# One waiting rule for a prefetched slab, and a weight split moved up on VectorE, in a two-block transformer kernel on one core

## The chip, the cores and the metric

The kernel runs on one core of a Trainium2 chip. The core has five engines with a queue of instructions each: TensorE (PE in the profile, with its weight loads as PEld), VectorE (DVE), ScalarE (ACT), GpSimd (POOL) and SyncE (SP), which in this kernel only issues DMAs. The engines meet through semaphores. The metric is the device time of one execution in microseconds, lower is better. Differences are judged against the kernel before, run on the same chip.

## The reference

Two transformer blocks in float32 over 256 tokens of width 1024. Cut to what matters here:

```python
# block 1
xn = rmsnorm(x, norm1_w)
gq, gk, gv, ggate, gr, mq, mk, mv = split(xn @ w_in)
o_gla  = rmsnorm(gla_chunked(gq, gk, gv, log_a), gla_out_norm_w) * silu(ggate)   # 4 heads
o_moba = moba_attention(rope(rmsnorm(mq)), rope(rmsnorm(mk)), mv)                # 8 heads, causal
x = x + (concat(o_gla, o_moba) * mix_scale) @ w_out
x = x + peer_ffn(rmsnorm(x, norm2_w), ...)        # 128 x 128 experts, top 16 of 8 heads
# block 2, for l in (0, 1): all of its scales and shifts come from
mod = silu(c) @ ada_w[l] + ada_b[l]               # 1024 x 6144 for each l
x = layer_norm(ALPHA * x + g1 * mixer(modulate(x, sh1, sc1)))
x = layer_norm(ALPHA * x + g2 * mlp(modulate(x, sh2, sc2)))
```

The product `silu(c) @ ada_w` depends on nothing that block 1 computes. The kernel computes pieces of it, called ada rows below, between the steps of block 1.

## The kernel before, in words

**Weights.** Every weight matrix comes in tiles of 128x1024 floats (512 KB). SP loads tile n into one of four places of `raw`, once tile n-4 has been split (`load`, L369). ACT rounds each half tile (128x512) to `w_hi` (`hi`, run under L1114), DVE computes the rest `w_lo = raw - w_hi` (`lo`, L1613), and TensorE multiplies three products of hi and lo parts (L497, L498). `w_hi` and `w_lo` hold four halves. DVE signals each finished half on `lo_done`.

**The ada rows.** One ada row (512 outputs) needs four slabs of `ada_w` of 128x1024 floats, slabs 4k to 4k+3 for row k. They lie in a ring of `ADA_RING = 4` places in `route`. `ada(k, ...)` (L574) makes eight products of 512 columns, two for each slab; before the first product of a slab TensorE waits for that slab's DMA (`ada_full`), and after it `ada_started` is counted up by one; after the eighth product of the row, `ada_row_full` is counted up by one. So `ada_started >= m` says that the first product of slab m-1 is done, and `ada_row_full >= k+1` that row k is done. `load_ada(n)` (L381 to L388) on SP waits until the slab's place is free and issues its DMA:

```python
if n % ADA_BATCH == ADA_BATCH - 1:
    sp.wait_ge(s["ada_row_full"], n // ADA_BATCH)       # fourth slab of a row: the row before is done
else:
    sp.wait_ge(s["ada_started"], n + 2 - ADA_RING)      # slab n-3 has begun, so slab n-4 is done
```

Rows 0 to 5 (slabs 0 to 23) run in block 1. SP's queue is strictly in order and mixes slabs with weight tiles: slabs 4 to 7 stand between the second and the third tile of `gg`, slabs 8 to 11 between the second and the third tile of `mv`, slabs 12 to 15 between the second and the third tile of `w_out`, slabs 16 to 23 ahead of the last four tiles of `w_out`.

**Order on TensorE, stage by stage.** ... ada row 0, `mk` projection, state updates (L670), rope rotations (L676), **ada row 1**, `gg` projection, gated linear attention output (`go`, L691 and L698), **ada row 2**, `mv` projection, then the softmax attention over four units of two heads (u = 0 to 3). For a unit, `moba_scores` (L735, L738), `moba_transposes` (L748) and `moba_values` (L764, L767). Between these stand **ada row 3** in two halves, the products `gbc` (L776) for the norm of the linear attention, and **rows 4 and 5** in halves. `ada_columns` (L567) and the `w_out` projection follow.

**Order on DVE in that last stage.** `moba_shifted(u)` (L1768 to L1775) scales and masks the scores and takes the maximum; ACT then does the exponentials; `moba_scaled(u)` (L1781, L1785) divides by the sum and releases the transposes of unit u on TensorE. L1807 multiplies the linear attention by `gbc` and frees the four PSUM banks of `gbc` (two of which the transposes of unit 0 take, the other two the scores of unit 2); L1814 applies the gate. `mixed_low` (L1792) and `moba_mixed` (L1798) prepare the input of `w_out`. The program is written out by hand; there is no scheduler.

Of the kernel before, what the change touches and what calls it, by code (L numbers as in the profile page):

```python
# [38 lines left out]
ADA_RING = 4  # L39
ADA_BATCH = 4  # L40
# [13 lines left out]
def columns(*sized):  # L54

    at, where = 0, {}
    for name, n in sized:
        where[name] = (at, n)
        at += n
    return where, at  # L60
# [14 lines left out]
TILE, NTILE = columns(("gq", 2), ("gk", 2), ("gr", 1), ("gv", 4), ("mq", 4), ("mk", 4), ("gg", 4), ("mv", 4),  # L75
                      ("w_out", KC), ("wq", 16), ("u", P), ("v", P),
                      ("aq", 4), ("ak", 4), ("bq", 4), ("bk", 1), ("av", 4), ("bv", 1), ("w_out2", KC),
                      ("mlp0", 64), ("conv_u", 16), ("conv_gate", 8), ("conv_out", KC), ("mlp1", 64))
# [46 lines left out]
def build(nc, ins, out):  # L125
    with ExitStack() as ctx:
# [26 lines left out]
        s = {name: ctx.enter_context(nc.semaphore(name)) for name in SEMS}  # L153
        raw_full = [ctx.enter_context(nc.semaphore(f"raw_full{i}")) for i in range(RAW)]
        ada_full = [ctx.enter_context(nc.semaphore(f"ada_full{i}")) for i in range(ADA_RING)]
# [4 lines left out]
        def V(name, i=0):  # L160
            return vec[:, VEC[name][0] + i:VEC[name][0] + i + 1]
# [27 lines left out]
        def C1(name):  # L189
            return con1[:, CON1[name][0]:CON1[name][0] + CON1[name][1]]  # L190
# [83 lines left out]
        ada_w = route[:, 0:ADA_RING * D]  # L274
# [3 lines left out]
        ada_slots = [ada_w[:, k * D:(k + 1) * D] for k in range(ADA_RING)]  # L278
# [11 lines left out]
        def use(name, k=0):  # L290
            n = USE[name][0] + k
            return n % NBANK, n // NBANK

        def B(name, k=0):
            return bank[use(name, k)[0]]

        def wait_full(eng, name, k=0, more=0):
            b, n = use(name, k)
            eng.wait_ge(bank_full[b], more + (n + 1))

        def wait_freed(eng, name, k=0, more=0):

            b, n = use(name, k)
            eng.wait_ge(bank_free[b], more + (n + 1))
# [23 lines left out]
        def free(name, k=0):  # L328
            return bank_free[use(name, k)[0]]

        def unit(n, half):

            a = (2 * n + half) % UNITS * HALF
            return slice(a, a + HALF)
# [10 lines left out]
        def ada_slot(n):  # L345

            r = n if n < ADA_1 * ADA_BATCH else n - ADA_GATES * ADA_BATCH
            return r % ADA_RING, r // ADA_RING
# [20 lines left out]
        def _(sp):  # L369
# [8 lines left out]
                for q in range(q0, TILE[name][1] if q1 is None else q1):  # L378
                    load(name, q, src[first + q])

            def load_ada(n, slot_free=False):  # L381
                if n >= ADA_RING and not slot_free:
                    if n % ADA_BATCH == ADA_BATCH - 1:
                        sp.wait_ge(s["ada_row_full"], n // ADA_BATCH)
                    else:
                        sp.wait_ge(s["ada_started"], n + 2 - ADA_RING)
                slot = ada_slot(n)[0]
                sp.dma_start(ada_slots[slot], ins["ada_w"][n]).then_inc(ada_full[slot], 16)  # L388

            def looped(name, src):  # L390
                with sp.Fori(0, TILE[name][1] // ROUND) as i:
# [7 lines left out]
            for name in ("gq", "gk", "gr", "gv", "mq", "mk"):  # L399
                straight(name, ins["w_in"], at)  # L400
                at += TILE[name][1]
                if name == "gv":
                    for n in range(ADA_RING):
                        load_ada(n)
            for n, name in enumerate(("gg", "mv")):
                straight(name, ins["w_in"], at, q1=2)
                for m in range(ADA_RING):
                    load_ada((n + 1) * ADA_RING + m)
                straight(name, ins["w_in"], at, q0=2)
                at += TILE[name][1]  # L410
            straight("w_out", ins["w_out"], q1=2)
            for n in range(3 * ADA_RING, 4 * ADA_RING):
                load_ada(n)
# [1178 lines left out]
        def _(dve):  # L1592
# [3 lines left out]
            def step(ins):  # L1596
                steps[0] += 1
                ins.then_inc(s["dve_step"], 1)
# [5 lines left out]
            def then_wait(ins):  # L1604
                step(ins)
                settle()

            def lo(n, i=0):

                for half in range(2):  # L1610
                    dve.wait_ge(s["hi_done"], i * (2 * ROUND) + (2 * n + half + 1))
                    a = n % RAW * D + half * HALF
                    v.tensor_tensor(w_lo[:, unit(n, half)], raw[:, a:a + HALF], w_hi[:, unit(n, half)].bitcast(F32),  # L1613
                                    ALU.subtract).then_inc(s["lo_done"], 1)
# [147 lines left out]
            def moba_shifted(u):  # L1762

                c = (u % 2) * 16
                for m in range(2):
                    a = (u % 2) * 6 * P + m * 3 * P
                    wait_full(dve, f"mp{u}", m)
                    v.scalar_tensor_tensor(sm1[:, a:a + 3 * P], B(f"mp{u}", m)[:, 0:3 * P], HD ** -0.5, C1("causal"),  # L1768
                                           ALU.mult, ALU.add).then_inc(free(f"mp{u}", m), 1)
                for m in range(2):  # L1770
                    wait_freed(dve, f"mp{u}", m)
                both = sm1[:, (u % 2) * 6 * P:(u % 2 + 1) * 6 * P].rearrange("p (m c) -> p m c", m=2)
                step(v.tensor_reduce(smx[:, c:c + 2], both[:, :, 0:P], AX, ALU.max))
                then_wait(v.tensor_reduce(smx[:, c + 2:c + 4], both[:, :, P:3 * P], AX, ALU.max))
                v.tensor_scalar(smx[:, c + 4:c + 8], smx[:, c:c + 4], -1.0, None, ALU.mult).then_inc(s["sm1_max"], 1)  # L1775

            def moba_scaled(u):

                c = (u % 2) * 16
                dve.wait_ge(s["sm1_exp"], u + 1)  # L1780
                then_wait(v.reciprocal(smx[:, c + 12:c + 16], smx[:, c + 8:c + 12]))  # L1781
                both = sm1[:, (u % 2) * 6 * P:(u % 2 + 1) * 6 * P].rearrange("p (m c) -> p m c", m=2)
                for n, part in enumerate((both[:, :, 0:P], both[:, :, P:3 * P])):
                    w = part.shape[2]
                    last = v.tensor_tensor(part, part, smx[:, c + 12 + 2 * n:c + 14 + 2 * n].unsqueeze(2).to_broadcast([P, 2, w]), ALU.mult)  # L1785
                last.then_inc(s["sm1_p"], 1)
# [12 lines left out]
                    .then_inc(s["chunk_t"], 1)  # L1799

            moba_shifted(0)
            moba_shifted(1)
            moba_scaled(0)
            for hd in range(GLA_H):
                a = slice((hd % 2) * 512 + (hd // 2) * T, (hd % 2) * 512 + (hd // 2) * T + T)
                wait_full(dve, "gbc", hd)
                v.tensor_tensor(mixed[:, hd * T:(hd + 1) * T], o_gla[:, a], B("gbc", hd)[:, 0:T], ALU.mult)\  # L1807
                    .then_inc(free("gbc", hd), 1)
            for hd in range(GLA_H):
                a = slice(hd * T, (hd + 1) * T)  # L1810
                if hd % 2 == 0:
                    wait_freed(dve, "gg", hd // 2)
                wait_freed(dve, "gbc", hd)
                v.scalar_tensor_tensor(mixed[:, a], mixed[:, a], V("mix", hd), gg[:, a], ALU.mult, ALU.mult).then_inc(s["chunk_t"], 1)  # L1814
            moba_shifted(2)
            moba_scaled(1)
            lo(TILE["w_out"][0] + 1)
            for c in range(4):
                mixed_low(c)
            moba_shifted(3)  # L1820
# [648 lines left out]
```

## Time and profile before

| | us |
|---|---|
| median of 3 executions | 1798.35 |
| lowest, highest | 1795.98, 1800.77 |
| the profiled execution: its time | 1800.77 |
| the profiled execution: span from first to last instruction | 1799.0 |

| engine | busy us | share | instructions |
|---|---|---|---|
| PE | 1704.0 | 95% | 11514 |
| DVE | 1215.2 | 68% | 2417 |
| ACT | 951.3 | 53% | 1830 |
| POOL | 77.2 | 4% | 74 |

The span is the time between the first and the last instruction of the profiled execution; about 1.8 us of its own time lie outside it. Busy shares are means over the whole span, with very different stages under them, so a local change is read in its own stage: here the stretch from 60 to 160 us. The granted clock of TensorE is 0.984 of full over the span.

### The profile page before, as it was taken

To read this page: it belongs to the slowest core of one execution; us is meant where nothing else is said; L and a number is where in the kernel's file an instruction comes from. 1 tells how busy PE (TensorE), PEld (TensorE's weight loads), DVE (VectorE), ACT (ScalarE), POOL (GpSimd) and SP (SyncE) were. 2 spreads that over 40 slices of the span, in tenths; PEclk is the share of its full clock that TensorE was granted. 3 is DMA by queue.
4 is the path that set the end of the run, shared out by engine and by line. 5 is a ranking of instruction groups with operands and counts; after the bars stand their busy time and mean duration, and the time that the engine had idled before them with its cause. 6 is when DMAs were issued, how large, how long until landed. Compare 5 with 4: busy or idle time off the path is not lost.

```text
span 1799.0 us, 33460 instructions
## 1 busy us (share of the span) xinstructions
PE 1704.0 (95%) x11514; PEld 1511.0 (84%) x11514; DVE 1215.2 (68%) x2417; ACT 951.3 (53%) x1830; POOL 77.2 (4%) x74
## 2 busy tenths in 40 slices
PE   7999999999999888999999999988999999889997
PEld 6767999999999755688888888867899979889996
DVE  5556568878854599866666676467676666767666
ACT  5445454554554588555555564346554445445443
POOL 0000000000000166200000000000000000000000
PEclk9989999999999899999999999999999999999999
DMA  6654445555555587565665654400365554445553
GB/s 235 213 206 166 146 151 181 175 186 175 176 185 180 194 291 281 190 195 191 203 208 191 193 192 138 163 24 14 118 187 186 187 208 150 149 137 188 187 188 101
DMA packets 86934, 316.35 MB, mean 176 GB/s; under 512 B 9664, under 2 KB 9808, under 8 KB 86352
## 3 DMA queue, kind: packets, MB, share of 16 engines
q1 hardware_dynamic: 85248, 309.30, 52.6%
q10 hardware_dynamic: 1328, 4.01, 0.6%
q0 software_dynamic: 288, 2.10, 0.3%
q8 instruction: 45, 0.74, 0.2%
q14 instruction: 25, 0.20, 0.0%
HBM read 314.32 MB, written 1.05 MB: 175 GB/s over the span
## 4 chain that ended last, share of the span: by engine, by line
PE 88%; DVE 6%; issue 2%; ACT 2%; DMA 1%; ACTq 0%; POOLq 0%; DVEq 0%; SPq 0%
PE bank L497 31%; PE acc L497 21%; PE bank L498 15%; PE acc L498 10%; PE bank L855 4%; PE acc L574 2%; PE bank L595 1%; ACT arena L1114 1%; DVE w_lo L1613 1%; DVE small L2110 1%; ACT w_hi L1114 1%; PE bank L814 0%; ACT L1114 0%; DVE arena L2131 0%; PE acc L980 0%
## 5 line engine op out<-in xcount | busy, mean ns | idle before, releaser
L1613 DVE TENSOR_TENSOR w_lo<-raw,w_hi 128x512 fp32r<-128x512 f32 x982 | 652.4, 689 | 421.6 <-ACT w_hi L1114 419.8
L1114 ACT ACTIVATE w_hi<-raw 128x512 fp32r<-128x512 f32 x982 | 592.5, 627 | 389.8 <-PE acc L497 239.1
L497 PE MATMUL bank<-x_hi,w_hi 128*128 128x256 f32 x2224 | 636.2, 286 | 23.2 <-DVE w_lo L1613 16.2
L497 PE MATMUL bank<-x_lo,w_hi 128*128 128x256 f32 x2224 | 632.3, 284 | 0.0
L498 PE MATMUL bank<-x_hi,w_lo 128*128 128x256 f32 x2224 | 632.1, 284 | 0.0
L497 PEld LDWEIGHTS bank<-x_hi,w_hi 128*128 128x128 f32 x2224 | 429.1, 193 | 30.7 <-issue 16.1
L497 PEld LDWEIGHTS bank<-x_lo,w_hi 128*128 128x128 f32 x2224 | 429.4, 193 | 0.8 <-issue 0.2
L498 PEld LDWEIGHTS bank<-x_hi,w_lo 128*128 128x128 f32 x2224 | 429.2, 193 | 0.0
L1114 ACT ACTIVATE arena<-bank 128x256 f32<-128x256 f32 (+4 forms) x172 | 89.6, 527 | 293.2 <-PE bank L498 291.6
L497 PE MATMUL acc<-w_hi,x_hi 128*128 128x512 f32 x560 | 219.3, 392 | 3.9 <-DVE w_lo L1613 2.5
L497 PE MATMUL acc<-w_lo,x_hi 128*128 128x512 f32 x560 | 218.4, 390 | 0.0
L498 PE MATMUL acc<-w_hi,x_lo 128*128 128x512 f32 x560 | 218.2, 390 | 0.0
L497 PEld LDWEIGHTS acc<-w_hi,x_hi 128*128 128x128 f32 x560 | 105.3, 188 | 30.5 <-issue 5.0
L498 PEld LDWEIGHTS acc<-w_hi,x_lo 128*128 128x128 f32 x560 | 105.3, 188 | 21.9
L497 PEld LDWEIGHTS acc<-w_lo,x_hi 128*128 128x128 f32 x560 | 105.3, 188 | 21.2
L855 PEld LDWEIGHTS bank<-route 128*128 128x128 f32 x512 | 62.8, 196 | 50.3 <-issue 50.2
L1574 POOL TENSOR_TENSOR route<-route,small 128x512 f32<-128x512 f32 x64 | 71.8, 1123 | 661.9 <-DVE route L1956 661.9
L497 PE MATMUL acc<-w_hi,tail_r 128*128 128x512 f32 x256 | 99.9, 390 | 0.0
L497 PE MATMUL acc<-w_lo,tail_r 128*128 128x512 f32 x256 | 99.9, 390 | 0.0
L498 PE MATMUL acc<-w_hi,tail_r 128*128 128x512 f32 x256 | 99.7, 389 | 0.0
L855 PE MATMUL bank<-route 128*128 128x128 f32 x512 | 71.7, 290 | 19.0 <-issue 17.5
L1956 DVE TENSOR_TENSOR route<-con,small 128x512 f32<-128x512 f32 x83 | 79.1, 971 | 0.0
(257 smaller groups left out, 1554.9 us busy)
## 6 DMA issues: line engine op xcount, KB each, us to landing
raw<-in_peer_u SPq DMA_DIRECT2D x128, 512.0 KB, 3.5
raw<-in_peer_v SPq DMA_DIRECT2D x128, 512.0 KB, 3.6
raw<-in_mlp_w SPq DMA_DIRECT2D x128, 512.0 KB, 3.5
ada_x<-in_ada_w SPq DMA_DIRECT2D x64, 512.0 KB, 4.1
route<-in_ada_w SPq DMA_DIRECT2D x32, 512.0 KB, 5.5
raw<-in_w_in SPq DMA_DIRECT2D x25, 512.0 KB, 4.5
raw<-in_conv_w_in SPq DMA_DIRECT2D x24, 512.0 KB, 4.1
raw<-in_attn_w_in SPq DMA_DIRECT2D x18, 512.0 KB, 3.4
```

Source lines behind the costliest of these rows:

```text
L497: return (mm(dst, a[0], b[0], start=start, stop=False, **kw), mm(dst, a[0], b[1], start=False, stop=False, **kw), mm(dst, a[1], b[0], star ...
L498: mm(dst, a[1], b[0], start=False, stop=stop, **kw))
L574: return mm(row[g:g + ADA_COLS, :], sc[:, a:a + ADA_COLS], w, start=start, stop=False, skip_group_check=True)
L595: last = mm(ps[:, 0:T], C("mean_d"), src[:, c, :], start=(c == 0), stop=(c == KC - 1))
L855: last = mm(ps[:, t * P:(t + 1) * P], jone[:, b:b + P], ione[:, a:a + P], start=True, stop=True)
L1114: return nc.scalar.activation(dst, src, f, **kw)
L1574: nc.gpsimd.tensor_tensor(e, e, gT[:, bass.ds(i * 32 + 4 * g, 4)].unsqueeze(2).to_broadcast([P, 4, P]), ALU.mult).then_inc(s["gated_i"], 1)
L1613: v.tensor_tensor(w_lo[:, unit(n, half)], raw[:, a:a + HALF], w_hi[:, unit(n, half)].bitcast(F32), ALU.subtract).then_inc(s["lo_done"], 1)
L1956: return v.tensor_tensor(dst.rearrange("p (t k) -> p t k", t=4), C("iota").unsqueeze(1).to_broadcast(shape), index[:, bass.ds(token, 4)].u ...
L2110: step(v.tensor_reduce(smx[:, c + m:c + m + 1], B(f"sc{n}_{m}")[:, :], AX, ALU.max))
```

## The change

Two edits. First, `load_ada` waits by one rule for every slab: `ada_started >= n-2`. (Its new argument `i` is never given and adds zero.) Second, on DVE the split of the second `w_out` tile moves from behind `moba_scaled(1)` to behind `moba_shifted(0)`, and `moba_scaled(0)` moves behind the four multiplications by `gbc`.

```diff
-            def load_ada(n, slot_free=False):
+            def load_ada(n, i=0, slot_free=False):
                 if n >= ADA_RING and not slot_free:
-                    if n % ADA_BATCH == ADA_BATCH - 1:
-                        sp.wait_ge(s["ada_row_full"], n // ADA_BATCH)
-                    else:
-                        sp.wait_ge(s["ada_started"], n + 2 - ADA_RING)
+
+                    sp.wait_ge(s["ada_started"], i * ADA_RING + (n + 2 - ADA_RING))
                 slot = ada_slot(n)[0]
-                sp.dma_start(ada_slots[slot], ins["ada_w"][n]).then_inc(ada_full[slot], 16)
+                sp.dma_start(ada_slots[slot], ins["ada_w"][i * ADA_RING + n]).then_inc(ada_full[slot], 16)
...
             moba_shifted(0)
+            lo(TILE["w_out"][0] + 1)
             moba_shifted(1)
-            moba_scaled(0)
             for hd in range(GLA_H):
...
+            moba_scaled(0)
             for hd in range(GLA_H):
...
             moba_shifted(2)
             moba_scaled(1)
-            lo(TILE["w_out"][0] + 1)
             for c in range(4):
                 mixed_low(c)
```

SP's queue around the slabs of rows 1 to 5, with what each DMA waits for; first before, then after. `route<-in_ada_w` is a slab, `raw<-in_w_in` and `raw<-in_w_out` are weight tiles.

```order
L375 DMA raw<-in_w_in 128x1024 [waits lo_done] x10
L388 DMA route<-in_ada_w 128x1024 [waits ada_started] x3
L388 DMA route<-in_ada_w 128x1024 [waits ada_row_full]
L375 DMA raw<-in_w_in 128x1024 [waits lo_done] x4
L388 DMA route<-in_ada_w 128x1024 [waits ada_started] x3
L388 DMA route<-in_ada_w 128x1024 [waits ada_row_full]
L375 DMA raw<-in_w_in 128x1024 [waits lo_done] x2
L375 DMA raw<-in_w_out 128x1024 [waits lo_done] x2
```

```order
L375 DMA raw<-in_w_in 128x1024 [waits lo_done] x10
L386 DMA route<-in_ada_w 128x1024 [waits ada_started] x4
L375 DMA raw<-in_w_in 128x1024 [waits lo_done] x4
L386 DMA route<-in_ada_w 128x1024 [waits ada_started] x4
L375 DMA raw<-in_w_in 128x1024 [waits lo_done] x2
L375 DMA raw<-in_w_out 128x1024 [waits lo_done] x2
```

No DMA changes its place; the fourth slab of each row waits for another semaphore. The order on TensorE is the same before and after.

VectorE in the attention stage, from `moba_shifted(0)` on; first before, then after (line numbers are lower by two). The TENSOR_TENSOR into `w_lo` is the weight split, the row with `arena,bank 128x256 x4` the multiplications by `gbc`.

```order
L1775 TENSOR_SCALAR small<-small 128x4
L1768 SCALAR_TENSOR_TENSOR arena<-bank,arena 128x384 x2
L1773 TENSOR_REDUCE small<-arena 128x2
L1774 TENSOR_REDUCE small<-arena 128x2
L1775 TENSOR_SCALAR small<-small 128x4
L1781 RECIPROCAL small<-small 128x4
L1785 TENSOR_TENSOR arena<-arena,small 128x2x128
L1785 TENSOR_TENSOR arena<-arena,small 128x2x256
L1807 TENSOR_TENSOR arena<-arena,bank 128x256 x4
L1814 SCALAR_TENSOR_TENSOR arena<-arena,vec 128x256 x4
```

```order
L1773 TENSOR_SCALAR small<-small 128x4
L1611 TENSOR_TENSOR w_lo<-raw,w_hi 128x512 x2
L1766 SCALAR_TENSOR_TENSOR arena<-bank,arena 128x384 x2
L1771 TENSOR_REDUCE small<-arena 128x2
L1772 TENSOR_REDUCE small<-arena 128x2
L1773 TENSOR_SCALAR small<-small 128x4
L1805 TENSOR_TENSOR arena<-arena,bank 128x256 x4
L1779 RECIPROCAL small<-small 128x4
L1783 TENSOR_TENSOR arena<-arena,small 128x2x128
L1783 TENSOR_TENSOR arena<-arena,small 128x2x256
L1813 SCALAR_TENSOR_TENSOR arena<-arena,vec 128x256 x4
```

Two splits and four multiplications now stand ahead of the scaling that releases the first transposes. No instruction is added or removed.

## Rows read from the trace of the kernel before

**Rows 1.** The page: engines of the chain that ended last.
```profile
PE 88%; DVE 6%; issue 2%; ACT 2%; DMA 1%; ACTq 0%; POOLq 0%; DVEq 0%; SPq 0%
```

**Rows 2.** Timeline of PE, the ada rows (start us, us, instruction, count).
```profile
84.21 1.92 PE L574 MATMUL acc<-route,small 128*32 128x512 f32 x16
...
107.04 3.64 PE L574 MATMUL acc<-route,small 128*32 128x512 f32 x16
...
127.41 1.07 PE L574 MATMUL acc<-route,small 128*32 128x512 f32 x8
...
129.27 1.06 PE L574 MATMUL acc<-route,small 128*32 128x512 f32 x8
130.26 1.27 PE L776 MATMUL bank<-arena,norm_rows 32*128 32x256 f32 x8
133.72 0.85 PE L748 MATMUL bank<-con,arena 128*128 128x128 f32 x6 [2.19 <-DVE arena L1807]
...
136.37 1.07 PE L574 MATMUL acc<-route,small 128*32 128x512 f32 x8
```

**Rows 3.** Timeline of SP's queue, 60 to 165 us.
```profile
69.81 2.03 SPq L388 DMA_DIRECT2D route<-in_ada_w  x4
72.30 15.89 SPq L375 DMA_DIRECT2D raw<-in_w_in  x4
88.24 1.94 SPq L388 DMA_DIRECT2D route<-in_ada_w  x4
```

**Rows 4.** Timeline of SP's queue, a narrow window: slab 20 alone.
```profile
137.51 0.33 SPq L388 DMA_DIRECT2D route<-in_ada_w  x1
```

**Rows 5.** DMA issues: 137.4 to 142.2 us, and all 32 slabs (L388).
```profile
route<-in_ada_w SPq DMA_DIRECT2D x1, 512.0 KB, 3.4
...
DMA to landing us min/median/max: 3.4/5.5/11.0
```

**Rows 6.** Timeline of ACT: the rounding of the third `gg` and `mv` tiles.
```profile
87.97 0.63 ACT L1114 ACTIVATE w_hi<-raw 128x512 fp32r<-128x512 f32 x1
...
113.89 1.17 ACT L1114 ACTIVATE w_hi<-raw 128x512 fp32r<-128x512 f32 x2
```

**Rows 7.** Timeline of DVE in the attention stage.
```profile
129.76 1.01 DVE L1768 SCALAR_TENSOR_TENSOR arena<-bank,arena 128x384 f32<-128x384 f32 x2
...
132.01 0.17 DVE L1781 RECIPROCAL small<-small 128x4 f32<-128x4 f32 x1
...
133.16 1.41 DVE L1807 TENSOR_TENSOR arena<-arena,bank 128x256 f32<-128x256 f32 x4
134.48 1.67 DVE L1814 SCALAR_TENSOR_TENSOR arena<-arena,vec 128x256 f32<-128x256 f32 x4
136.07 1.02 DVE L1768 SCALAR_TENSOR_TENSOR arena<-bank,arena 128x384 f32<-128x384 f32 x2
...
139.46 1.29 DVE L1613 TENSOR_TENSOR w_lo<-raw,w_hi 128x512 fp32r<-128x512 f32 x2
```

**Rows 8.** The chain that ended last, in order of time.
```profile
143.19 5.58 DMA route<-in_ada_w
148.81 1.05 PE acc L574 x4
```

**Rows 9.** Stretches: us, busy time of PE, PEld, DVE, ACT, POOL, clock, DMA.
```profile
101.50:110.60 9.10, 9.10 (x36) 4.94 (x34) 0.00 (x0) 0.00 (x0) 0.00 (x0) 0.50 0.00 0
...
41.60:50.00 8.40, 5.78 (x25) 4.43 (x24) 4.26 (x7) 6.31 (x15) 0.00 (x0) 1.00 0.77 267
...
612.80:616.10 3.30, 0.03 (x1) 0.03 (x1) 1.18 (x4) 1.92 (x3) 0.00 (x0) 1.00 0.83 278
616.10:627.20 11.10, 9.61 (x37) 4.97 (x38) 8.89 (x15) 8.12 (x23) 7.00 (x6) 0.54 0.56 202
...
181.10:183.60 2.50, 0.02 (x1) 0.00 (x0) 2.38 (x5) 0.81 (x2) 0.00 (x0) 0.96 0.07 26
183.60:187.00 3.40, 3.35 (x16) 3.38 (x17) 3.40 (x10) 1.81 (x5) 0.00 (x0) 0.52 0.02 5
```

## Prediction

> **What bounds the kernel now.** I read the page first. TensorE holds 88% of the chain that ended last and DVE 6%, DMA 1% [rows 1]: a microsecond added to TensorE's queue anywhere on that chain ends up in the time, one added elsewhere only if TensorE comes to wait for it. Then I read the timeline of TensorE in the stage that the change touches. The eight products of ada row 1 run without a pause from 84.21 to 86.1 us, those of row 2 from 107.04 to 110.7 us [rows 2]. SP's queue shows why: the four slabs of row 1 were issued together at 69.81 us, those of row 2 at 88.24 us [rows 3], 14 and 19 us ahead of their use. In the attention stage the reader is to see two other things: TensorE waits 2.19 us for DVE at 133.72 us [rows 2], and the chain later passes through one DMA, slab 23, issued at 143.19 us and landed 5.58 us later, after which TensorE goes on at 148.81 us [rows 8].
>
> **The change part by part: the wait.** The fourth slab of row k is slab n = 4k+3. Before, it waits until row k-1 is done. After, it waits for `ada_started >= n-2 = 4k+1`, and that count is reached only when the first product of row k itself is done. So TensorE begins row k, this releases the DMA of the slab that row k needs for its seventh product, and TensorE comes to that product long before the slab. A prefetch turns into a fetch on demand.
>
> Row 1. From the first product of a slab to the issue on SP: row 4 begins at 136.37 us, its second slab about a quarter of the two-slab half later, at 136.9 us by two products of 0.27 us each, and slab 20, which waits for that, is issued at 137.51 us [rows 2, 4]: 0.6 us. Slab 20 landed 3.4 us after its issue, alone on the queue; the median of all slabs is 5.5 us [rows 5]. Row 1 begins at 84.21 us, so slab 7 is issued at 84.8 us and lands at 88.2 us at the earliest. Its product is due at three quarters of the 1.9 us, at 85.6 us. The stall is 2.6 us, with a lag 0.5 us longer 3.1, with the median landing 4.7. I take 2.9, near the lone slab, because the queue stands still ahead of slab 7: everything issued at 69.81 us has landed.
>
> Row 2. This row ran at half the clock (0.50 from 101.5 to 110.6 us [rows 9]): 3.64 us for the eight products, the seventh due at 2.7 us. The first product takes 0.2 us more than at full clock, so slab 11 lands at 0.8 + 3.4 = 4.2 us after the start: 1.5 us of stall, up to 2.0 with the longer lag, 4.1 with the median landing. I take 1.8. Were the clock at full there, it would be as in row 1.
>
> What is queued behind the waiting DMA on SP: at slab 7 the last two `gg` tiles and the first two of `mv` (issued from 72.30 us before [rows 3], now from about 85.3), at slab 11 the last two `mv` tiles and two of `w_out`. ACT rounds the third `gg` tile at 87.97 us [rows 6] on TensorE's release, which moves with the stall to about 90.9; the tile is issued second behind slab 7, at about 85.3, and with the median landing of 5.5 us is there at 90.8. ACT takes the third `mv` tile at 113.89 us [rows 6], 6.8 us after row 2 began, 8.6 after the stall; the tile, issued some 1.3 us after row 2 begins and behind one slab, is there at 6.8. Both are covered, the first with nothing to spare; if this cover fails, each costs up to 1 us, which I keep in the upper bound.
>
> Row 3: slab 15 is issued at 127.41 + 0.6 = 128.0 us and lands at 131.4, while the seventh product was due at 129.8 (the half begins at 129.27 [rows 2]). TensorE pauses 1.6 us, the `gbc` products (1.27 us at 130.26 [rows 2]) end at 133.1 instead of 131.5. But TensorE then waits for DVE until 133.72 anyway, longer after the change (below): I count 0, and 1.3 us if the slab takes its 5.5 us. Row 4: slab 19 has the whole of unit 1's transposes and scores between its issue and its use: 0. Row 5: slab 23 now follows the first product of row 5, which itself comes later by the DVE term below, so it is issued some 2 us after the 143.19 us of before [rows 8], but with less queued ahead of it; this is in the next term.
>
> **The moved split and scaling.** Before, `moba_shifted(1)` runs from 129.76 to 132.01 us, the scaling of unit 0 from 132.01 to 133.16, the `gbc` multiplications from 133.16 to 134.48, and TensorE starts its transposes at 133.72, as soon as the first multiplication has freed a bank [rows 2, 7]. After, two splits (1.29 us for two at 139.46 [rows 7]) come first: `moba_shifted(1)` ends at 133.3, the multiplications (1.32) at 134.6, the scaling (1.15) at 135.8. The transposes of unit 0 start at about 135.9, 2.2 us later. Unit 2's scores follow them; DVE comes to `moba_shifted(2)` at 135.8 + 1.6 = 137.4 instead of 136.07 [rows 7], and finds the scores at about 137.6: 135.9 plus 0.85 for the transposes plus 0.9, half of what lies between the transposes' end and row 4 in [rows 2]. That is 1.5 us late. From there the scaling of unit 1 and its transposes are 1.5 us late, and with them the products that release slabs 21 and 22. The split that has left this place gives DVE 1.2 us back only after the transposes of unit 1 are released, and there the chain is on TensorE and slab 23 [rows 8], not on DVE. So the stage ends 1.5 us late by DVE, up to 2.3 by slab 23; I take 1.8. Below: if the two splits fell fully into waits, 0.5 remains for the order of scaling and multiplication.
>
> **The clock.** Pauses of TensorE sometimes take the granted clock down to half, 1.2 GHz. After the pause of 2.5 us at 181.1 the dense matmuls ran at 0.52 for 3.4 us; after 3.3 us at 612.8 it was 0.54 for 11 us; but over the 8.4 us from 41.6, of which TensorE was busy for only 5.8, it stayed at 1.00 [rows 9]. The pause in row 1 is of this size and stands ahead of the dense `gg` projection. I take one such stretch of 3.4 us, of which half, 1.7 us, is lost; the bounds are 0 and, by the longer stretch, 5.1 more than the sum.
>
> The Trainium skill (TensorE: Matmul & The Clock Gate, section "HAM oscillation — how this bites in real kernels") tells of a kernel in which every wait for a DMA between short bursts sent the array back to the lower clock. This trace agrees at 181.1 us and disagrees at 41.6 us [rows 9]. By that rule row 1 and row 2 would both pay; by the rows alone I count one of the two. The rule's result is the first rival.
>
> Sum: 2.9 + 1.8 + 1.8 + 1.7 = 8.2 us. Against the profiled execution's own 1800.77 us this would be 1809.0. That execution is the slowest of the three shown, so I put the sum on the median: 1798.35 + 8.2 = 1806.6 us.
>
> **Rivals.** (a) Each new pause takes the clock down. For it: the rows at 181.1 and 612.8 us. Against it: the row at 41.6 us. Price: two stretches between 3.4 and 10 us at half clock, 1.7 to 5.1 us lost in each, so 6.5 + 3.4 to 10.2; in the middle 13 us, 1811.5 us.
>
> (b) Not slower: the slow stretch of before goes away. The linear attention output and row 2 ran at clock 0.50 from 101.5 to 110.6 us [rows 9], 9.1 us for work of 4.6 at full clock. The pause in row 1 moves this work by 2.9 us, and the clock may fall later, where TensorE waits anyway, or not at all. Then 4.6 us come back, row 2's stall is 2.9 instead of 1.8, and without the clock term the sum is 6.5 + 1.1 - 4.6 = 3.0 us: 1801.4, no change that can be measured. It decides once more than about 3 us of that slow stretch are gone. Against it: the work that stands ahead of the fall is the same.
>
> (c) The waits do not bite, because the slab is there in time. This would need 1.4 us from the release to the landing in row 1; the shortest landing of 32 is 3.4 us [rows 5]. Only the DVE term would be left, 1.8 us: 1800.2.
>
> **How the numbers follow.** About 0.3% (5.4 us) is what a measurement of this kernel can tell from no change. Forecast 0.62, (a) 0.15, (b) 0.15, (c) 0.04, and 0.04 for something that makes it faster. The forecast's own terms run from 2.6 + 1.5 + 0.5 = 4.6 without clock to 4.7 + 4.1 + 2.3 + 1.3 + 1 + 1.7 = 15.1 with all; the part of the forecast under 5.4 us is about 0.08 of the whole. Slower: 0.54 + 0.15 = 0.69, with the doubtful part to 0.72; same 0.24; faster 0.04. The range goes from (b) with some of its weight left out, 1801.5, to the middle of (a) and a little over, 1813.
>
> **What the profile would show.** TensorE waits in L574 for `route<-in_ada_w` once in rows 1 and 2 each, 2.5 to 3.5 us in row 1, released by a slab issued about 0.6 to 1.1 us after the row began. SP's queue shows the four slabs of row 1 no longer as one piece: three at about 70 us and one at about 85 us. The first transposes of unit 0 come 2 us later against the start of `moba_scores(0)`, with DVE's scaling as their releaser, and the `w_out` projection 1.5 to 2.3 us later. I am wrong if slab 7 is issued at 70 us, if row 1 has no pause, or if the part before 126 us costs nothing; a gain would have to come from the clock between 86 and 115 us.

## The result: slower by about 16 us, twice the forecast, and the profile after

| | us |
|---|---|
| before, median of 5 | 1798.35 |
| after, median of 5 (1809.77 to 1819.13) | 1815.79 |
| ratio | 1.0089, 95% interval 1.0064 to 1.0114 (+11.5 to +20.5) |
| forecast | 1806.6 (1801.5 to 1813.0) |

The change makes the kernel slower, and TensorE waits at the places forecast, but it is slower by 16.0 us (by the ratio) where 8.2 were summed. The time lies outside the range. The profiled execution after has a span of 1812.7 us.

The timeline of PE after, the ada rows (L572 is L574 of before), beside [rows 2]:

```profile
82.94 1.91 PE L572 MATMUL acc<-route,small 128*32 128x512 f32 x12
87.91 1.46 PE L572 MATMUL acc<-route,small 128*32 128x512 f32 x4 [3.06 <-DMA route<-in_ada_w]
...
111.70 3.63 PE L572 MATMUL acc<-route,small 128*32 128x512 f32 x12
117.26 1.05 PE L572 MATMUL acc<-route,small 128*32 128x512 f32 x4 [1.93 <-DMA route<-in_ada_w]
...
139.35 1.69 PE L572 MATMUL acc<-route,small 128*32 128x512 f32 x4 [1.90 <-DMA route<-in_ada_w]
140.97 1.24 PE L774 MATMUL bank<-arena,norm_rows 32*128 32x256 f32 x8
144.84 1.54 PE L746 MATMUL bank<-con,arena 128*128 128x128 f32 x6 [2.64 <-DVE arena L1783]
```

Each row of eight products is cut after its sixth, and the seventh waits for a DMA: 3.06 us in row 1, 1.93 in row 2, 1.90 in row 3. In [rows 2] none of these waits is there. The first transposes (L746) wait for the scaling (L1783), as forecast. A count of x16 is eight products, since each product of an ada row leaves two records.

SP's queue after, beside [rows 3]: the four slabs of a row are no longer one piece of 2 us. The pieces now hold the wait for the fourth slab, 15.8 us for row 1 and 22.3 us for row 2.

```profile
68.55 15.80 SPq L386 DMA_DIRECT2D route<-in_ada_w  x4
84.39 7.24 SPq L375 DMA_DIRECT2D raw<-in_w_in  x4
91.67 22.29 SPq L386 DMA_DIRECT2D route<-in_ada_w  x4
```

In a narrow window, slab 7's own issue, 1.08 us after row 1 began:

```profile
84.02 0.33 SPq L386 DMA_DIRECT2D route<-in_ada_w  x1
```

The same stages in stretches, first before, then after (columns: stretch, its length, busy time of PE, PEld, DVE, ACT, POOL, clock, DMA share, GB/s). The stages are row 1 to the end of `gg`; the small matmuls of the linear attention's output; row 2; `mv`; the attention stage.

```profile
84.21:97.99 13.78, 13.78 (x115) 12.22 (x115) 9.01 (x15) 7.89 (x12) 0.00 (x0) 1.00 0.73 284
97.99:107.04 9.05, 9.05 (x39) 7.16 (x38) 1.25 (x2) 1.00 (x2) 0.00 (x0) 0.69 0.25 84
107.04:110.61 3.57, 3.57 (x17) 0.59 (x16) 0.00 (x0) 0.00 (x0) 0.00 (x0) 0.50 0.00 0
110.61:126.56 15.95, 14.45 (x93) 10.74 (x89) 8.81 (x13) 10.42 (x19) 0.00 (x0) 0.96 0.61 230
126.56:153.01 26.45, 20.09 (x153) 9.47 (x153) 21.41 (x53) 14.64 (x49) 0.00 (x0) 1.00 0.55 199
```

```profile
82.94:102.33 19.39, 16.33 (x115) 13.44 (x115) 9.10 (x15) 7.98 (x12) 0.00 (x0) 0.91 0.59 218
102.33:111.70 9.37, 9.37 (x40) 7.38 (x39) 1.25 (x2) 1.00 (x2) 0.00 (x0) 0.67 0.01 2
111.70:118.24 6.54, 4.61 (x18) 0.71 (x17) 0.00 (x0) 0.00 (x0) 0.00 (x0) 0.69 0.48 179
118.24:133.68 15.44, 13.95 (x90) 10.33 (x89) 8.80 (x13) 10.41 (x19) 0.00 (x0) 1.00 0.51 196
133.68:165.49 31.81, 25.09 (x152) 10.77 (x152) 21.69 (x53) 14.52 (x49) 0.00 (x0) 0.84 0.59 216
```

Row 1 and what follows are 5.6 us longer, row 2 by 3.0, the attention stage by 5.4; the two others change by 0.3 and -0.5. That is 13.8 us of the span's 13.7. Two readings matter for what follows. The attention stage has 6.7 us of idle TensorE after and 6.4 before, nearly the same; what grew is its busy time, at a granted clock of 0.84 instead of 1.00. And row 1's stage holds 3.06 us of idle time but is 5.6 longer, at clock 0.91. (The stretch ahead of row 1, which the change does not touch, is 1.3 us shorter after. What lies behind the attention stage makes up for that.) The clock fell to half in the 3.4 us right behind row 1's pause:

```profile
88.40:91.80 3.40, 3.40 (x15) 2.50 (x12) 1.22 (x3) 1.57 (x2) 0.00 (x0) 0.50 0.72 293
```

### The profile page after: what moved, and what is told of

It is laid out like the page before. It is cut to its first block, busy times and chain, and to the rows that moved or that the text cites. A ratio compares the mean times of both kernels' runs of the same rounds, so it can differ in the third digit from the quotient of the medians.

```text
span 1812.7 us, 33460 instructions
## 1 busy us (share of the span) xinstructions
PE 1713.1 (95%) x11514; PEld 1514.5 (84%) x11514; DVE 1215.4 (67%) x2417; ACT 951.0 (52%) x1830; POOL 77.2 (4%) x74
## 4 chain that ended last, share of the span: by engine, by line
PE 88%; DVE 6%; issue 2%; ACT 2%; DMA 2%; ACTq 0%; POOLq 0%; DVEq 0%
PE bank L495 30%; PE acc L495 21%; PE bank L496 15%; PE acc L496 10%; PE bank L853 4%; PE acc L572 3%; PE bank L593 1%; ACT arena L1112 1%; DMA route<-in_ada_w 1%; DVE w_lo L1611 1%; DVE small L2108 1%; ACT w_hi L1112 1%; PE bank L812 0%; ACT L1112 0%; DVE arena L2129 0%
## 5 line engine op out<-in xcount | busy, mean ns | idle before, releaser
L495 PEld LDWEIGHTS bank<-x_hi,w_hi 128*128 128x128 f32 x2224 | 429.6, 193 | 29.1 <-issue 14.9
```

The lines of the kernel that those rows point to most:

```text
L495: return (mm(dst, a[0], b[0], start=start, stop=False, **kw), mm(dst, a[0], b[1], start=False, stop=False, **kw), mm(dst, a[1], b[0], star ...
```

## The experiments

Each was timed in five rounds beside the kernel before. Microseconds from a ratio are the ratio's excess times 1799.

**Both edits apart.** `w_only` is the kernel before with the new `load_ada` wait; `d_only` is the changed kernel with the old wait:

```diff
-                    sp.wait_ge(s["ada_started"], i * ADA_RING + (n + 2 - ADA_RING))
+                    if n % ADA_BATCH == ADA_BATCH - 1 and not (False):
+                        sp.wait_ge(s["ada_row_full"], n // ADA_BATCH)
+                    else:
+                        sp.wait_ge(s["ada_started"], n + 2 - ADA_RING)
```

> Only the new waiting rule for the fourth slabs; VectorE's order as before. Theory A (the pauses for slabs 7, 11 and 15 are the cause, and they also pull the clock down behind them): 11 to 15 us slower than before; row 1 pauses 3 us and row 2 about 2, and the granted clock falls to half once after row 1 and once in the attention stage. Theory B (the moved split and scaling on VectorE are what brought the attention stage from 26.4 to 31.8 us; the slab waits cost only their own 5 us): 5 to 7 us slower than before, attention stage within 1.5 us of the 26.4 us of before, clock there 1.00.

> Only the new order on VectorE; the waiting rule as before. Theory A: 1.5 to 2.3 us slower than before, not to be told from no change; attention stage 28 us at clock 1.00, with the first transposes 2.2 us later. Theory B: 5 to 8 us slower, attention stage 30 us or more with the clock down to half in it.

Measured: `w_only` 1.0075 (1.0062 to 1.0089), +13.5 us; `d_only` 1.0019 (1.0010 to 1.0029), +3.4 us. Together 16.9, the change 16.0: the edits add up within the intervals, and the wait is four fifths of it. The attention stage of `w_only`, then of `d_only`, and in `d_only` the first transposes:

```profile
133.24:163.06 29.82, 23.88 (x152) 10.60 (x152) 21.60 (x53) 14.51 (x49) 0.00 (x0) 0.89 0.64 230
```

```profile
126.39:156.30 29.91, 24.11 (x152) 11.30 (x152) 21.60 (x53) 14.63 (x49) 0.00 (x0) 0.83 0.49 177
```

```profile
135.66 1.54 PE L748 MATMUL bank<-con,arena 128*128 128x128 f32 x6 [3.09 <-DVE arena L1785]
```

Either edit alone lengthens this stage by 3.4 to 3.5 us, at a clock below 1.00. In `d_only` TensorE waits 3.09 us ahead of the transposes instead of 2.19. It has waited once more before that, inside the `gbc` products, for a bank that the masking of unit 1's scores frees behind the two splits:

```profile
131.41 1.16 PE L776 MATMUL bank<-arena,norm_rows 32*128 32x256 f32 x4 [0.61 <-DVE arena L1768]
```

The same six transposes then take 1.54 us instead of 0.85 [rows 2]. Neither theory stood as written. Theory A was right on `w_only`'s time. It was wrong on `d_only`'s clock, and wrong on a fall behind row 1: from row 1 to the end of `gg` the clock of `w_only` was 1.00 (17.54 us, from 85.14 us on). Theory B was wrong on `w_only`'s 5 to 7 us and on `d_only`'s 5 to 8.

**The wait, slab by slab.** The kernel before with the new wait for slab 7, for slab 11, or for slabs 15, 19 and 23 alone:

```diff
-                    if n % ADA_BATCH == ADA_BATCH - 1:
+                    if n % ADA_BATCH == ADA_BATCH - 1 and not (n == 7):      # or n == 11, or n > 11
```

> The kernel before, with the new wait for slab 7 alone. Theory A (as corrected by the profile after: slab 7 is issued 1.1 us into the row, lands 3.5 us later, and the last two products then take 1.0 us instead of ending with the rest): the row and what follows to the gg projection takes 3.8 us more, and the clock may or may not fall for 3.4 us behind it; 3.8 to 5.5 us slower than before. Rival (the pause costs only its 2.7 to 3.1 us, as in the prediction): 2.5 to 3.2 us slower. Second rival (the pause is made up later, because TensorE waits less for VectorE after it): within 1 us of before.

> The kernel before, with the new wait for slab 11 alone. Theory A: row 2 takes 3.0 to 3.3 us more than the 3.57 us of before, whether the clock is at half there or not; 3 to 4 us slower. Rival (the prediction's 1.8 us): 1.5 to 2.2 us slower.

> The kernel before, with the new wait for slabs 15, 19 and 23 alone. The prediction counted 0 for row 3 and 0 for row 4, and for row 5 a part of 0.5 us. Theory A (the pause in row 3 joins the wait for VectorE into one longer stretch of idle time and the clock falls in the attention stage): 3 to 5 us slower, attention stage about 29.8 us, clock there below 0.95. Rival (no fall): 0.5 to 1.5 us slower, attention stage below 28 us at clock 1.00.

Measured: slab 7 1.0030 (1.0018 to 1.0042), slab 11 1.0028 (1.0019 to 1.0037), the other three 1.0011 (1.0003 to 1.0020): 5.4, 5.0 and 2.0 us, 12.4 together against 13.5 of `w_only`. Row 1 in the profile of `row1_only`, on PE and on SP:

```profile
83.91 1.91 PE L574 MATMUL acc<-route,small 128*32 128x512 f32 x12
88.43 1.05 PE L574 MATMUL acc<-route,small 128*32 128x512 f32 x4 [2.61 <-DMA route<-in_ada_w]
```

```profile
84.99 0.33 SPq L388 DMA_DIRECT2D route<-in_ada_w  x1
```

The slab is issued 1.08 us after the row's start, lands 3.44 us later, and the last two products take 1.0 us until the next stage begins; the whole row of before took 1.85. That makes the step 3.7 us longer, as its stretch shows, at full clock:

```profile
83.91:101.35 17.44, 14.83 (x115) 12.35 (x115) 9.00 (x15) 7.90 (x12) 0.00 (x0) 1.00 0.85 322
```

So theory A's 3.8 holds for the step, and the whole time, 5.4 us, is at the upper end of its 3.8 to 5.5. In `row2_only` row 2 takes 6.57 us, 3.0 more than before, as in the changed kernel:

```profile
106.70:113.27 6.57, 4.62 (x17) 0.71 (x17) 0.00 (x0) 0.00 (x0) 0.00 (x0) 0.70 0.54 190
```

The time grew by 5.0 (3.4 to 6.7), above the 3 to 4 expected, though the interval takes in the upper part of that. In `rows345_only` the attention stage takes 31.39 us at clock 0.89, longer than either theory had it, but the time grew by only 2.0 us, between the two: this one execution gained 2.4 us in the two stages ahead, where its clock fell later than in the profile of before.

**Matmuls put into the pauses.** Products of 512 columns of constants, ahead of the seventh product of a row, which nobody reads:

```diff
+FILL = {1: 3, 2: 1, 3: 2}
...
                 for c in range(c0, c1):
...
+                    if c == 6 and k in FILL:
+                        if k == 3:
+                            pe.wait_ge(s["mv_ready"], 2)
+                        keep_busy(FILL[k], con, 512)
```

> The changed kernel, with matmuls on constants (their result is never read) put into the pauses ahead of the seventh product: three of 512 columns in row 1, one in row 2, two in row 3, about as long as the pause each. Theory A: TensorE's time in the pauses is the same as a wait, but the clock no longer falls behind row 1 and in the attention stage: 5 to 8 us faster than the changed kernel (about 8 to 11 us slower than before), the attention stage about 28 us. Rival (the clock falls by itself, from the small matmuls around the rows, whether TensorE pauses or not): as slow as the changed kernel, 16 to 19 us slower than before, with the same half-clock stretches.

Measured on the changed kernel: 1.0083 (1.0069 to 1.0097), +14.9 us against 16.0. Expected by theory A were 8 to 11. It can't be told from the changed kernel, so the fill of all three rows at once settled little; its attention stage still took 30.23 us at clock 0.94. The same was then asked of single rows, with and without the wait (`{1: 3}` and `{2: 1}`, without the two lines on `k == 3`):

> The kernel before, all waits as before, with three matmuls of 512 columns on constants ahead of the seventh product of row 1 (their result is never read): TensorE is busy as long there as it pauses in row1_only. If a delay on TensorE's chain ends up in the time one to one: the step from row 1 to the next stage is 3.6 to 3.7 us longer and the time 3 to 4.5 us longer. If a delay there costs more than itself, because it shifts all later work against the clock's falls: 5 us or more.

> row1_only with the same three matmuls in its pause. Theory A (idleness costs beyond its length): nearer to pad_row1 than row1_only is, and at least 1 us faster than row1_only (5.4 us slower than before by its ratio). Rival (the pause costs its length and nothing more, idle or busy): the same as row1_only and as pad_row1, within 1 us.

> The kernel before, all waits as before, with one matmul of 512 columns on constants ahead of the seventh product of row 2, where the clock is at half in most executions: the row takes 2.4 to 2.6 us more. One to one: 2 to 3 us slower. If the step's surroundings add to it, as in row2_only (step 3.0 us longer, time 5.0 us longer by its ratio): 4 us or more.

> row1_only once more, beside row2_filled, since its first interval rests on 6 runs. If the idle pause costs beyond its length: ratio again 1.0025 or more (4.5 us), against 1.0014 and 1.0016 of row1_filled and pad_row1. If not: 1.0013 to 1.0020.

> row2_only with one matmul of 512 columns in its pause of 1.9 us. Row 2's step 3.0 us longer as in row2_only. If idle time costs extra: 2.5 to 3.5 us slower than before, 1.5 us less than row2_only (ratio 1.0028). If any delay there costs the same: ratio 1.0025 to 1.003.

| | wait | filler | step longer by, us | ratio (95%) | us |
|---|---|---|---|---|---|
| row1_only | yes | no | 3.7 | 1.0030 (1.0018 to 1.0042) | 5.4 |
| row1_again | yes | no | 3.8 | 1.0029 (1.0016 to 1.0041) | 5.2 |
| row1_filled | yes | yes | 3.8 | 1.0014 (1.0004 to 1.0024) | 2.5 |
| pad_row1 | no | yes | 3.7 | 1.0016 (1.0007 to 1.0025) | 2.9 |
| row2_only | yes | no | 3.0 | 1.0028 (1.0019 to 1.0037) | 5.0 |
| row2_filled | yes | yes | 3.0 | 1.0024 (1.0015 to 1.0034) | 4.3 |
| pad_row2 | no | yes | 2.3 | 1.0016 (1.0006 to 1.0025) | 2.9 |

The step of row 1 is equally long in its four kernels, but where TensorE idled in it the kernel was 5.3 us slower on average, and where it was busy 2.7. The repeats of each kind agree. The evidence is thin all the same: each single interval takes in the step's own 3.7 us, the two averages are 2.6 us apart, give or take about 2 (an estimate from the four intervals), and the idle and the busy kernels were not timed side by side, each only beside the kernel before. The stretch from row 1 to the end of `gg` in `pad_row1`, with nearly the same length as in `row1_only` above:

```profile
81.61:99.13 17.52, 17.52 (x121) 13.39 (x121) 9.00 (x15) 7.89 (x12) 0.00 (x0) 1.00 0.60 228
```

The clock is 1.00 in this stretch with and without filler, so no fall follows row 1's pause there. What differs in the profiles lies 40 us later, in the attention stage, where these kernels have the same work. `row1_only`, then `row1_filled`, then `pad_row1`:

```profile
128.53:156.19 27.66, 21.38 (x152) 10.42 (x152) 21.50 (x53) 14.88 (x49) 0.00 (x0) 0.94 0.51 191
```

```profile
127.94:154.28 26.34, 19.81 (x152) 9.46 (x153) 21.42 (x53) 14.65 (x49) 0.00 (x0) 1.00 0.55 201
```

```profile
126.19:152.40 26.21, 21.39 (x152) 9.89 (x152) 21.42 (x53) 14.65 (x49) 0.00 (x0) 0.93 0.57 201
```

`row1_again` repeats `row1_only` (27.64 us at 0.94). From the start of row 1 to the end of the attention stage the profiles of the two idle kernels are 3.5 and 3.7 us longer than that of before (68.80 us), those of the two busy ones 2.3 and 2.0. So the profiles show 1.2 to 1.7 us of the 2.6, all of it in the attention stage. The rest is not seen in them.

Row 2 doesn't repeat the difference: filled or not, it costs 4.3 to 5.0, and the filler alone 2.9 for a step of 2.3. In the one profile of `row2_only` the same long stretch is only 2.5 us longer than before (71.33 us), so its 5.0 us are not seen there either.

**VectorE's edits apart, and filled.** The split alone moved up; the scaling alone moved behind the multiplications; and `d_only` with three filler products ahead of the first transposes.

```diff
+            pe.wait_ge(s["mv_ready"], 2)
+            keep_busy(3, con, 512)
             moba_transposes(0)
```

> Only the split of the second w_out tile moved up. Theory A: first transposes 1.2 us later than in before, stage 27.2 to 27.7 us at clock 1.00; 1 us slower, not to be told from no change. Rival (it brings the clock down as both edits together did): 29 us or more.

> Only the scaling of unit 0 moved behind the four multiplications. Theory A: the transposes now wait for the scaling, 0.9 us later than in before; the second unit's maximum is not later, since its scores are ready only then, up to 0.5 us; 0.3 to 1 us slower, no change that can be measured. Rival (clock): 2 us or more slower.

> The new order on VectorE alone, as in d_only, with three matmuls of 512 columns on constants put ahead of the first transposes of the attention stage, where TensorE waited 3.1 us (their result is never read). Theory A (the longer wait takes the clock down): the clock stays at 1.00 in the attention stage, which takes 28.0 to 28.5 us instead of 29.9; 1 to 2 us faster than d_only. Rival (the clock falls from the sparse work of the whole stage, not from that wait): half-clock stretch all the same, stage 29.5 us or more, no faster than d_only.

Measured: the split 1.0003 (0.9994 to 1.0012), the scaling 0.9994 (0.9985 to 1.0003), no change either; filled 1.0020 (1.0010 to 1.0029), the same as `d_only`. The attention stages of the split, the scaling and the filled kernel:

```profile
122.27:149.91 27.64, 22.05 (x152) 10.38 (x153) 21.59 (x53) 14.58 (x49) 0.00 (x0) 0.94 0.53 191
```

```profile
126.45:153.94 27.49, 21.57 (x153) 10.17 (x153) 21.50 (x53) 14.43 (x49) 0.00 (x0) 0.94 0.53 193
```

```profile
126.68:155.82 29.14, 24.73 (x158) 11.01 (x159) 21.59 (x53) 14.40 (x49) 0.00 (x0) 0.94 0.51 181
```

Here theory A on the single edits holds for the time and for the stage's length (about 1 us more each), though not for the clock, which it had at 1.00. Its claim for the filler falls: busy matmuls in the wait did not make the kernel faster. The clock fell later in the stage instead, and the stage stayed 2.7 us longer than before. Whether the two edits cost more together than apart is not shown: by the upper ends of their intervals (2.2 and 0.5 us) they make up 2.7, and the interval of `d_only` begins at 1.8.

**Another order around the linear attention's output**, meant to test the clock and, if it held, to beat the kernel before:

```diff
-            for hh in range(2):
+            def go_half(hh):
...
-            ada(2, acc[0], 2)
+            go_half(0)
...
-            project_rows("mv", [acc[2][:, :], acc[3][:, :]], tiles_of_tokens, s["mv_full"], head_squares)
+            project_rows("mv", [acc[2][:, :], acc[3][:, :]], tiles_of_tokens, s["mv_full"],
+                         {1: lambda: go_half(1), 2: head_squares, 3: lambda: ada(2, acc[0], 2)})
```

> The kernel before with another order on TensorE, to test the clock itself: the two halves of the linear attention's output (small matmuls of 64 and 128 columns) stand apart, with the first mv tile between them, and row 2 stands ahead of the last mv tile instead of in front of the first. Theory A (a stretch of small or few matmuls is what brings the clock down at 101.5 us, for 10.2 us): the clock stays at 1.00 from 84 to 126 us, and the stretch from the start of row 1 to the attention stage takes 38 us instead of 42.4; 3 to 5 us faster than before. Rival (the fall has nothing to do with the work around it): the half-clock stretch comes all the same, no change or slower.

> The interleaved order on TensorE, and on VectorE the split of the second w_out tile later than before, behind mixed_low(4), where VectorE idles for 2.5 us. If VectorE bounds the second half of the attention stage: 0.5 to 1.2 us faster than interleaved. If TensorE and slab 23 bound it (the prediction's reading of the chain): the same as interleaved, 2 to 3 us faster than before.

The numbers say ahead of which of the four `mv` tiles the work stands, counted from 0.

Measured: 0.9983 (0.9974 to 0.9992), 3.1 us faster than before (1.4 to 4.7), and 0.9986 (0.9977 to 0.9995) with the later split, the same. The stretch that took 28.57 us before (97.99 to 126.56, at clock 0.82) now, with the same work in it:

```profile
96.76:121.06 24.30, 22.80 (x143) 15.98 (x143) 10.15 (x15) 11.53 (x21) 0.00 (x0) 1.00 0.34 118
```

It is 4.3 us shorter at full clock, as expected, and 3.1 of that are in the time. TensorE idles 1.50 us in it both before and after, so the gain is the clock's. The two interleaved kernels are the fastest of this study. That the later split changed nothing fits the chain of [rows 8], on which VectorE no longer stands in the second half of the attention stage.

## Why the prediction was wrong

**What held.** The waits are where they were put, at the seventh product of rows 1 and 2; slab 7 is issued when row 1 begins; the weight tiles behind the waiting slabs were covered (ACT took the third `gg` tile at the release of TensorE). Rival (c), that the slab is in time, is out. Rival (b), the slow stretch going away, did not come: the stage of small matmuls took 9.37 us at clock 0.67. The first transposes came with DVE's scaling as releaser. Forecast, terms and measurement:

| term | forecast, us | step in the profile, us | time alone, us |
|---|---|---|---|
| row 1 | 2.9 | 3.7 and 3.8 | 5.4 and 5.2 |
| row 2 | 1.8 | 3.0 | 5.0 |
| rows 3, 4, 5 | 0, a part for row 5 in the next term | 1.8 (first transposes, `rows345_only`) | 2.0 |
| VectorE | 1.8 | 2.1 (first transposes, `d_only`) | 3.4 |
| clock | 1.7 | | in the rows above |
| sum | 8.2 | 10.6 without clock | 15.8 (the change: 16.0) |

The times alone of rows 1 and 2 lie even above the largest values that the text had for them, 4.7 and 4.1.

**The step that failed: how a row runs.** The prediction read a row as eight products one after another, about 0.24 us each. The trace of before shows four products side by side, each in two overlapping passes of 0.6 us, 1.04 us from a product's start to its end. (`ada_product` puts four successive products on four different groups of 32 columns.) Row 1 of before in a window of 0.3 us, the half row in front of slab 20 in a narrow window, and the fifth and sixth product of row 1 in `row1_only`, which run as a pair:

```profile
84.21 0.64 PE L574 MATMUL acc<-route,small 128*32 128x512 f32 x4
```

```profile
136.37 0.64 PE L574 MATMUL acc<-route,small 128*32 128x512 f32 x4
```

```profile
84.79 0.60 PE L574 MATMUL acc<-route,small 128*32 128x512 f32 x2
```

Six products therefore take 1.91 us, as long as all eight. The prediction's row 1 term went wrong in three places by this. The lag of 0.6 us was counted from 136.9 us, where the second slab's first product was thought to begin, but it began with the others at 136.38; from there to the issue of slab 20 it is 1.1 us, as in rows 1 and 3 (1.08). The seventh product was put at three quarters of the row, 1.4 us in, but TensorE is only done with six at 1.9 us. These two errors cancel: the pause of 2.61 us in `row1_only` meets the 2.6 of the working by luck. The third error has nothing to cancel it: once slab 7 is there, the last two products take 1.0 us until the next stage, where before they ran beside the fifth and sixth and added nothing to the row's 1.85. 1.08 + 3.44 + 1.0 - 1.85 is the 3.7 us that were measured; 2.9 was forecast. The landing of 3.4 us [rows 5] was right.

**Row 2.** The same, with the first six products at half the clock. Slab 11 is issued 1.95 us after the row's start, where the text had 0.8:

```profile
108.65 0.33 SPq L388 DMA_DIRECT2D route<-in_ada_w  x1
```

It lands 3.64 us later, and the last two products, at full clock again, take 0.98 us: 1.95 + 3.64 + 0.98 - 3.57 is the step of 3.0. The pause, 1.96 us, was near the 1.8 forecast, again because the lag and the due time were both too early. The 2 us of time beyond the step are open. They are not idleness in the row (filled or not, the same), and each interval reaches down to 3.4 or less.

**Row 3.** The text let its pause vanish in the wait for VectorE. In `rows345_only` slab 15 is issued 1.08 us after row 3 began and lands 4.6 us later, where 0.6 and 3.4 were assumed. The `gbc` products are done 3.5 us later in the stage than before, more than the 2.19 us of cover, and the first transposes start 1.8 us later:

```profile
128.77 1.05 PE L574 MATMUL acc<-route,small 128*32 128x512 f32 x4 [2.76 <-DMA route<-in_ada_w]
...
131.24 1.51 PE L748 MATMUL bank<-con,arena 128*128 128x128 f32 x6 [0.56 <-DVE arena L1807]
```

The time grew by 2.0 us (0.5 to 3.6); the upper bound for this term was 1.3. In the changed kernel the two edits also meet here: the multiplications by `gbc` now stand ahead of the scaling, and `gbc` comes after row 3's second half, so the pause of row 3 holds up DVE:

```profile
142.22 1.41 DVE L1805 TENSOR_TENSOR arena<-arena,bank 128x256 f32<-128x256 f32 x4 [1.79 <-PE bank L774]
```

That row is DVE's timeline after. The products of `gbc` began 6.4 us after row 3 instead of 2.9 and missed DVE's slot. The first transposes start 4.0 us later in the stage than before, which is about the 1.8 of row 3 and the 2.1 of VectorE's edits together. (In this profile slab 15 landed 3.7 us after its issue and the clock fell with row 3's last two products.)

**VectorE.** The first transposes came later by 2.1 us against the stage's start (9.27 us in `d_only`, 7.16 before), the 2.2 of the working. The time's 3.4 us (1.8 to 5.2) takes in the 1.8 forecast at its lower edge. The excess shows in the profiles as the stage's clock: 0.83.

**The clock.** The forecast gave 1.7 us for one half-clock stretch, placed behind the pause of row 1. In the profile of the changed kernel that stretch came, at 88.40 us, behind a pause of 3.06 us. In `w_only`, `row1_only` and `row1_again`, behind pauses of 2.61 to 2.79 us, it did not: their clock stayed at 1.00 to the end of `gg`. Whether the longer pause or the moment made the difference is open. An estimate for the whole change comes from the recorded span and clock of every execution, as the span times one minus the clock: 32.3 us on average in the changed kernel, 27.8 in the kernel before beside `w_only`. At most 4.5 us of the 16 are then the clock's, against 1.7 forecast. With the 10.6 us of the steps that gives about 15. For row 1 alone the same estimate shows nothing: against their own kernels before, the two idle ones lost 0.8 more and 0.6 less, the two busy ones 0.2 more and 0.9 less. Between row 1's step of 3.7 us and its time of 5.3, what the profiles show is the fall in the attention stage (about 1.3 us). Why it falls there, and the remainder, stay open.

**Rival (a)**, each pause takes the clock down, was nearest in its time (1811.5, range 9.9 to 16.7 us against 16.0 measured), but as a mechanism it did not hold: it wanted a fall behind each pause, which three of the four profiles with row 1's pause lack, and filling the pauses of all three rows, and the wait of VectorE's edit, did not bring the time back. The rule of the Trainium skill (TensorE: Matmul & The Clock Gate, section "HAM oscillation — how this bites in real kernels"), that waits for DMAs between short bursts bring the array down, agrees with the changed kernel at row 1 (0.50 from 88.40 us) and not with `row1_only` (1.00 over the same work). The two waits that the prediction set beside that rule, at 181.1 and 41.6 us, were for VectorE (2.5 us each) and not for a DMA. So the nearness of the rival's time is in part luck: of the 8 us that the forecast lacked, about 4 are longer steps (10.6 against 6.5), and at most 3 are clock.

## What to carry to other kernels

A prefetch whose release is the first instruction of its own consumer is no prefetch. For every slab of a ring, ask which instruction releases it and how far that stands ahead of the use; write the difference down in microseconds. A fetch on demand costs the release's lag, the landing, and the tail of work that no longer overlaps, not just the idle time that the trace will show. Before dividing a row's time by its number of products, look in a narrow window whether they run side by side: here four did, a product lasted four times as long as the division said, and two left over cost 1.0 us. And price the clock as a range for the whole change, not as a stretch behind a certain pause. It pays to look where small matmuls stand in a row: putting a dense tile between two groups of them gave 3.1 us here with no instruction added.

## What the hardware showed that was not expected

- The clock's falls in the attention stage come and go between kernels with the same work there. Of the eight profiles in which this stage is untouched and nothing before it is reordered, three show 1.00 (before, `row1_filled`, `row2_only`) and five 0.87 to 0.94. The profile of before is one of the three, so a stage beside it looks a little worse than it is.
- What a fall costs depends on what it meets. In `pad_row1` it began before TensorE's second wait for VectorE in this stage, that wait shrank to 0.59 us from the 2.17 of before, and the stage took 26.21 us against 26.45 with no fall. In `row1_only` an equally long fall began when that wait was over, and the stage took 27.66.

```profile
139.24 0.87 PE L751 MATMUL bank<-con,arena 128*128 128x128 f32 x6 [0.59 <-DVE arena L1788]
```

```profile
141.56 1.54 PE L748 MATMUL bank<-con,arena 128*128 128x128 f32 x6 [2.16 <-DVE arena L1785]
```

- In the profile of before the clock fell to half in the midst of the small matmuls (64 and 128 columns) of the linear attention's output, with TensorE busy without a gap since 84.21 us, and stayed there for 10.2 us. With a dense tile between their two halves it stayed at 1.00 in that stretch, in both interleaved kernels.
- The slowest and the fastest execution of one kernel lie 3.3 to 9.4 us apart. A stage's length in one profile (31.39 us in `rows345_only`, 5 more than before) can be far from its share of the median time (2.0 us).
